# A delta rule kernel: order of work in the first and the last of eight heads

## The chip, the cores and the metric

The kernel runs on one core of one Trainium2 chip. The metric is the device time of one execution, in microseconds (us). Three runs of the kernel before gave 2688.31, 2688.33 and 2689.46 us; the median, 2688.33 us, is what the changed kernel is held against.

## The reference

The program is a trunk of two layers over 1024 tokens of width 1024: a gated DeltaNet mixer and a feed-forward block, then a gated linear attention mixer and a second feed-forward block. The change lies in the first mixer. Cut to that part, with the normalisation and the convolution named only:

```
qkv = silu(causal_depthwise_conv(p[..., :GDN_QKV], conv_w))       # 4 taps
q, k = l2_norm(q) * dk ** -0.5, l2_norm(k)
gc = cumsum(g)                                                     # in each chunk
decay = exp(where(causal, gc[i] - gc[j], -inf))
a = where(strict, (k * beta) @ k.T * decay, 0)
u, w = triangular_solve(a + eye, [v * beta, k * beta * exp(gc)])
qk = where(causal, q @ k.T * decay, 0)
for each chunk:                                                    # the scan
    v_new = u - w @ state
    o = (q * exp(gc)) @ state + qk @ v_new
    state = state * exp(gc_end) + (k * exp(gc_end - gc)).T @ v_new
o = rms_norm(o) * silu(z);  return o @ w_out
```

There are 8 heads of width 128. All arithmetic is float32; the large products are made from two rounded parts of each operand, as three matrix products.

## The kernel before, in words

One function, `gdn`, holds the mixer. It writes one program for each engine by hand, and the engines meet at semaphores; nothing reorders them, so the order of the code is the order of the queues. Each program runs `body(0)`, a loop of `body(h)` for heads 1 to 6, `body(7)` and `after(8)`. `peeled(h)` is true for head 0 and `final(h)` for head 7, so code under them is in one head only.

A head needs four projections of the input: keys, queries, values and the gate z. Each is a 1024x1024 weight tile in SBUF. SyncE loads it (`load(h, k)`), ScalarE rounds it to the high part (`high(h, k)`), GpSimd makes the low part (`split(h, k)`), and TensorE multiplies. TensorE's share is cut into pieces called fills: `fill(h, n)` is 6 matmuls of 512 columns. Fills 8k to 8k+7 make projection k of head h in PSUM (`pa`), four fills for each half of the tokens; projection 0 is the queries, 1 the values, 2 the next head's keys, 3 the gate z. (Head 0's fills -8 to -1 are its own keys; fills 0 to 7 its queries.) The first fill of each half waits until ScalarE has evicted that half of `pa` (`evict(h, k, half)`, semaphore `s_u`).

Beside the fills run the steps of the delta rule:

- VectorE convolves the keys in four taps (`conv`), ScalarE applies silu, TensorE turns them by token (`keys_by_token`), ScalarE squares them and copies them (`key_squares`), VectorE sums, ScalarE takes the root (`key_deviation`), and VectorE makes factors and multiplies the decay matrix (`key_chain`). TensorE multiplies the keys with themselves (`key_products`); VectorE makes the coupling matrix `aT` from both (`coupling_matrix`).
- The decay matrix starts from the row sums of the log decays. TensorE turns them (`decay_rows`), VectorE copies them (`cumT`), SyncE stores them to memory and loads them back, spread over all partitions (`load_columns`), and ScalarE takes two exponentials (`decay_exps`).
- The triangular inverse: GpSimd copies small blocks of `aT` (`near_blocks`), VectorE inverts them in some 25 small steps (`near_turned` to `near_back`), GpSimd spreads the result (`spread`, tiles `first` and `firstT`). Then three joins double the block: TensorE makes `coupled(h, n)`, ScalarE copies it (`m1_copies(h, n)`), TensorE makes `joined(h, n)`, VectorE subtracts (`join(h, n)`).
- Then query-key products, values by token, the product with w, and the next head's keys.

In head 7 the gate z takes the place of projection 2. Its tile `zc` still holds the output of head 6 until a DMA has stored it, so `evict(7, 2, 0)` waits for that store (semaphore `s_ost`).

Of the kernel before, what the change touches and what calls it, by code (L numbers as in the profile page):

```python
# [1144 lines left out]
GDN_TAPS = 4  # L1145
# [302 lines left out]
def gdn(nc, consts, w_in, w_gates, conv_w, a_log, dt_bias, o_gain, x_hi, x_lo, x_raw, mixed, cum_rows, w_out, x_in, x_out,  # L1448
# [3 lines left out]
    with ctx:  # L1452
# [128 lines left out]
        def peeled(h):  # L1581
            return isinstance(h, int) and h == 0
# [181 lines left out]
        def _(act):  # L1764
# [60 lines left out]
            def scan(h, projects, scans):  # L1825
                beside = {} if projects else tail_beside()
                if projects:
                    beside = {0: lambda: high(h, 1),
                              1: lambda: evict(h, 0, 0),
                              3: lambda: (evict(h, 0, 1), high(h, 2)),  # L1830
                              5: lambda: evict(h, 1, 0)}
# [44 lines left out]
            def prepare(h):  # L1876
# [14 lines left out]
                act.activation(stdq[:, :], ssq[:, :], ACT.Sqrt, bias=eps[:, 0:1]).then_inc(s_qstd, 1)  # L1891
                evict(h, 2, 0)
                m1_copies(h, 1)
                if not peeled(h):
                    silu(vT, 3 * h + 3)
# [44 lines left out]
            evict(0, -1, 1)  # L1940
            decay_exps_of_gates()
            silu(kT, 1)
            decay_exps(0)
            key_squares(0)
            key_deviation(0)
# [28 lines left out]
        def _(dve):  # L1974
# [17 lines left out]
            def conv_q(h, some):  # L1992
                conv(qT, u[1], 3 * h, halves(h, 0, 1), some)
# [138 lines left out]
            def scan(h, projects, scans):  # L2132
                beside = {}
                if projects:
# [7 lines left out]
                    if peeled(h):  # L2142
                        beside[0] = lambda: (coupling_matrix(h), conv_q(h, (1, 2, 3)))
                        beside[4] = lambda: near_joined(h, True)
                        del beside[6]
                for n in range(NT):
# [79 lines left out]
            def make_gates():  # L2226
# [31 lines left out]
                                  gates[:, :, G_CUM, :], ALU.subtract).then_inc(s_gr, 1)  # L2258
                dve.wait_ge(s_cumTp, 1)
                dve.tensor_copy(cumT[:, :], cumT_ps).then_inc(s_cumT, 1)  # L2260

            make_gates()
            dve.wait_ge(s_taps, 32)
            dve.wait_ge(s_set, 1)
            conv(kT, u[0], 1, halves(0, -1, 1), range(GDN_TAPS))
            dve.wait_ge(s_gates, 1)
# [23 lines left out]
        def _(pe):  # L2290
# [124 lines left out]
            def prepare(h):  # L2415
# [4 lines left out]
                if peeled(h):  # L2420
                    fill(h, *range(16, 24))
                pe.wait_ge(s_first, 2 * h + 2)
# [16 lines left out]
                coupled(h, 1)  # L2439
                some(20)  # L2440
                joined(h, 1)
                some(21, 22)
                coupled(h, 2)
                some(23)
                joined(h, 2)
# [810 lines left out]
```

## Time and profile before

| what | value |
|---|---|
| median of three runs | 2688.33 us |
| the profiled execution's own time | 2685.92 us |
| its span | 2683.9 us |
| mean granted TensorE clock | 0.991 of full speed |
| TensorE busy in matmuls | 2599.2 us (97%) |
| VectorE, GpSimd, ScalarE busy | 61%, 44%, 42% |
| first head, first projection to the loop over heads | about 31 to 131 us |
| last head, after its share of the scan, to the tail | about 638 to 681 us |

The profiled execution took 2.4 us less than the median; 2.0 us of its time lie outside the span. In a row of the timeline the first number is the start, the second the duration (of all instructions of a merged row, from the first's start to the last's end), both in us from the start of the span; then come the engine, the line, the operation, the tiles and the shape. What stands in square brackets is the time that the engine sat idle ahead of it, and what ended that.

### The profile page before, as it was taken

What the parts mean: (1) busy time and instruction counts of PE and PEld (TensorE: products, weight loads), DVE (VectorE), ACT (ScalarE), POOL (GpSimd) and SP (SyncE); (2) the same over time, 40 slices, a digit from 0 to 9 for tenths busy, and PEclk for the clock granted to TensorE, in tenths of its full rate; (3) what the DMA queues carried; (4) which work ended last, traced back from release to release, by engine and by line L of the source; (5) the groups of instructions that cost most, each with busy time, mean ns of one, the idle gap of its engine ahead of it and who ended that gap; (6) DMA issues with size and microseconds to landing.
All of it is one profiled execution on the core that took longest, in us unless ns stands there. A gap on an engine that the chain in (4) does not pass through costs nothing. (4 is left out here: it accounts for less than half of the span.)

```text
span 2683.9 us, 34327 instructions
## 1 busy us (share of the span) xinstructions
PE 2599.2 (97%) x12821; PEld 2156.9 (80%) x12821; DVE 1636.2 (61%) x1740; ACT 1115.2 (42%) x1645; POOL 1179.1 (44%) x721
## 2 busy tenths in 40 slices
PE   6999999999989999999999999999989999999998
PEld 5788888888778888888888688888878888888887
DVE  5677666676168666665455658557448666665454
ACT  6445545544443443433244334434533443433242
POOL 3444333434404778784443111111413877774442
PEclk9999999999999999999999999999999999999999
DMA  3111011111432222225554111012522222234553
GB/s 120 35 38 47 31 39 47 42 36 42 124 114 101 79 85 79 87 80 168 174 175 135 61 36 48 23 55 69 160 87 78 87 71 94 71 105 154 169 189 113
DMA packets 84541, 238.07 MB, mean 89 GB/s; under 512 B 8928, under 2 KB 22816, under 8 KB 84416
## 3 DMA queue, kind: packets, MB, share of 16 engines
q1 hardware_dynamic: 84416, 236.39, 26.6%
q8 instruction: 80, 1.31, 0.2%
q14 instruction: 45, 0.37, 0.0%
HBM read 189.66 MB, written 46.69 MB: 88 GB/s over the span
## 5 line engine op out<-in xcount | busy, mean ns | idle before, releaser
L391 POOL TENSOR_TENSOR f_wlo<-f_raw,f_whi 128x512 fp32r<-128x512 f32 (+1 forms) x210 | 426.5, 2032 | 499.4 <-ACT f_whi L432 499.4
L703 DVE TENSOR_TENSOR f_hlo<-f_hraw,f_hhi 128x512 fp32r<-128x512 f32 x88 | 182.1, 2075 | 200.9 <-ACT f_hhi L490 200.9
L432 ACT ACTIVATE f_whi<-f_raw 128x512 fp32r<-128x512 f32 (+1 forms) x210 | 171.9, 834 | 274.5 <-PE f_value L75 252.7
L391 POOL TENSOR_TENSOR f_wlo<-f_sums,f_whi 128x512 fp32r<-128x512 f32 x144 | 188.2, 1317 | 39.8 <-ACT f_whi L432 39.8
L432 ACT ACTIVATE f_whi<-f_sums 128x512 fp32r<-128x512 f32 x144 | 90.3, 627 | 270.7 <-POOL f_sums L397 270.7
L73 PE MATMUL f_value<-x_hi,f_whi 128*128 128x512 f32 x416 | 162.6, 391 | 1.6 <-POOL f_wlo L391 1.6
L74 PE MATMUL f_value<-x_lo,f_whi 128*128 128x512 f32 x416 | 162.6, 391 | 0.0
L75 PE MATMUL f_value<-x_hi,f_wlo 128*128 128x512 f32 x416 | 162.5, 391 | 0.0
L73 PE MATMUL f_part<-f_whi,f_hhi 128*128 128x512 f32 x352 | 137.9, 392 | 0.0
L75 PE MATMUL f_part<-f_whi,f_hlo 128*128 128x512 f32 x352 | 137.5, 391 | 0.0
L74 PE MATMUL f_part<-f_wlo,f_hhi 128*128 128x512 f32 x352 | 137.1, 389 | 0.0
L1685 POOL TENSOR_TENSOR g_wlo_first<-g_raw_first,g_whi_first 128x1024 fp32r<-128x1024 f32 x15 | 36.7, 2447 | 203.9 <-ACT g_whi_first L1770 203.9
L698 DVE TENSOR_TENSOR f_kept<-f_part,f_kept 128x512 f32<-128x512 f32 x72 | 49.8, 692 | 108.7 <-ACT f_kept L482 103.2
L2694 POOL TENSOR_TENSOR l_wlo<-l_raw,l_whi 128x1024 fp32r<-128x1024 f32 x12 | 29.3, 2445 | 195.3 <-ACT l_whi L2723 195.3
L73 PE MATMUL banks<-x_hi,g_whi 128*128 128x512 f32 x256 | 109.1, 426 | 6.2 <-POOL g_wlo L1685 6.2
L73 PE MATMUL banks<-x_hi,g_whi_first 128*128 128x512 f32 x256 | 110.1, 430 | 3.9 <-POOL g_wlo_first L1685 3.9
L75 PE MATMUL f_part<-x_hi,f_wlo 128*128 128x512 f32 x288 | 112.5, 390 | 0.0
L74 PE MATMUL f_part<-x_lo,f_whi 128*128 128x512 f32 x288 | 112.5, 390 | 0.0
L73 PE MATMUL f_part<-x_hi,f_whi 128*128 128x512 f32 x288 | 112.4, 390 | 0.0
L474 ACT ACTIVATE f_gate<-f_gate 128x1024 f32<-128x1024 f32 x44 | 46.7, 1062 | 148.5 <-DVE f_gate L689 148.5
L75 PE MATMUL banks<-x_hi,g_wlo_first 128*128 128x512 f32 x256 | 101.0, 395 | 0.0
L74 PE MATMUL banks<-x_lo,g_whi_first 128*128 128x512 f32 x256 | 100.9, 394 | 0.0
(539 smaller groups left out, 7652.2 us busy)
## 6 DMA issues: line engine op xcount, KB each, us to landing
f_raw<-in_ffn_w_up SPq DMA_DIRECT2D x88, 512.0 KB, 3.6
f_raw<-in_ffn_w_down SPq DMA_DIRECT2D x88, 512.0 KB, 3.6
hidden<-f_hid SPq DMA_DIRECT2D x44, 512.0 KB, 2.8
f_hraw<-hidden SPq DMA_DIRECT2D x88, 256.0 KB, 3.9
g_raw_first<-in_gdn_w_in SPq DMA_DIRECT2D x16, 512.0 KB, 3.6
g_raw<-in_gdn_w_in SPq DMA_DIRECT2D x16, 512.0 KB, 4.2
f_xt<-x_mid SPq DMA_DIRECT2D x16, 512.0 KB, 4.8
l_raw_first<-in_gla_w_in SPq DMA_DIRECT2D x12, 512.0 KB, 3.6
```

Source lines behind the costliest of these rows:

```text
L73: pe.matmul(out, w_hi, x_hi, start=first, stop=False)
L74: pe.matmul(out, w_hi, x_lo, start=False, stop=False)
L75: return pe.matmul(out, w_lo, x_hi, start=False, stop=last)
L391: pool.tensor_tensor(part_of(w_lo, k), source, part_of(w_hi, k).bitcast(F32), ALU.subtract) \
L432: act.activation(part_of(w_hi, k), source, ACT.Copy).then_inc(s_hi, 1)
L474: act.activation(gate[:, :], gate[:, :], ACT.Silu).then_inc(s_silu, 1)
L698: dve.tensor_tensor(out, psum, kept_part, ALU.add).then_inc(s_comb, 1)
L703: dve.tensor_tensor(h_lo[d % FFN_SLOTS][:, :], h_raw[d % HIDDEN_RAWS][:, :], plain32(h_hi[d % FFN_SLOTS][:, :]), ALU.subtract).then_inc(s_ ...
L1685: pool.tensor_tensor(w_lo[s][:, :], raw[s][:, :], w_hi[s][:, :].bitcast(F32), ALU.subtract) \
L2694: pool.tensor_tensor(w_lo[s][:, :], raw[s][:, :], w_hi[s][:, :].bitcast(F32), ALU.subtract) \
```

## The change

Six edits, all in `gdn`. In head 0: (1) VectorE's four taps for the keys are cut in two pairs, and the copy of the decay rows stands between them. (2) ScalarE's `high(0, 1)`, the rounding of the value weights, stands ahead of the silu of the keys; before, it stood after `key_deviation`. (3) `key_squares(0)` stands ahead of `decay_exps(0)`. (4) On VectorE two of the three remaining query taps move from behind the coupling matrix to behind `near_back`. (5) On TensorE fills 20 to 23 move from ahead of the joins to between them. In head 7: (6) ScalarE's copies for the second join stand ahead of the gate's first eviction.

```diff
--- before.py
+++ after.py
@@ -1825,7 +1825,7 @@
             def scan(h, projects, scans):
                 beside = {} if projects else tail_beside()
                 if projects:
-                    beside = {0: lambda: high(h, 1),
+                    beside = {0: lambda: None if peeled(h) else high(h, 1),
                               1: lambda: evict(h, 0, 0),
                               3: lambda: (evict(h, 0, 1), high(h, 2)),
                               5: lambda: evict(h, 1, 0)}
@@ -1889,8 +1889,11 @@
                     high(h, 3)
                 act.wait_ge(s_qss, h + 1)
                 act.activation(stdq[:, :], ssq[:, :], ACT.Sqrt, bias=eps[:, 0:1]).then_inc(s_qstd, 1)
-                evict(h, 2, 0)
+                if not final(h):
+                    evict(h, 2, 0)
                 m1_copies(h, 1)
+                if final(h):
+                    evict(h, 2, 0)
                 if not peeled(h):
                     silu(vT, 3 * h + 3)
                 if final(h):
@@ -1939,9 +1942,10 @@
             gate_exps()
             evict(0, -1, 1)
             decay_exps_of_gates()
+            high(0, 1)
             silu(kT, 1)
+            key_squares(0)
             decay_exps(0)
-            key_squares(0)
             key_deviation(0)
 
             def body(h):
@@ -2140,9 +2144,8 @@
                               5: lambda: near_back(h),
                               6: lambda: conv_q(h, (2, 3))}
                     if peeled(h):
-                        beside[0] = lambda: (coupling_matrix(h), conv_q(h, (1, 2, 3)))
+                        beside[0] = lambda: (coupling_matrix(h), conv_q(h, (1,)))
                         beside[4] = lambda: near_joined(h, True)
-                        del beside[6]
                 for n in range(NT):
                     if scans and n < NT - 1:
                         update_state(h - 1, n)
@@ -2256,13 +2259,14 @@
                 dve.drain()
                 dve.tensor_tensor(g_abs[:, :, :], total_ps.rearrange("p (h c) -> p h c", h=H),
                                   gates[:, :, G_CUM, :], ALU.subtract).then_inc(s_gr, 1)
-                dve.wait_ge(s_cumTp, 1)
-                dve.tensor_copy(cumT[:, :], cumT_ps).then_inc(s_cumT, 1)
 
             make_gates()
             dve.wait_ge(s_taps, 32)
             dve.wait_ge(s_set, 1)
-            conv(kT, u[0], 1, halves(0, -1, 1), range(GDN_TAPS))
+            conv(kT, u[0], 1, halves(0, -1, 1), (0, 1))
+            dve.wait_ge(s_cumTp, 1)
+            dve.tensor_copy(cumT[:, :], cumT_ps).then_inc(s_cumT, 1)
+            conv(kT, u[0], 1, halves(0, -1, 1), (2, 3))
             dve.wait_ge(s_gates, 1)
             key_chain(0)
 
@@ -2418,7 +2422,7 @@
                         fill(h, *fills)
 
                 if peeled(h):
-                    fill(h, *range(16, 24))
+                    fill(h, *range(16, 20))
                 pe.wait_ge(s_first, 2 * h + 2)
                 pe.wait_ge(s_at, h + 1)
                 coupled(h, 0)
@@ -2437,11 +2441,11 @@
                 else:
                     pe.wait_ge(s_qsq, h + 1)
                 coupled(h, 1)
-                some(20)
+                fill(h, 20)
                 joined(h, 1)
-                some(21, 22)
+                fill(h, 21, 22)
                 coupled(h, 2)
-                some(23)
+                fill(h, 23)
                 joined(h, 2)
                 fill(h, 24)
                 query_key_products(h)
```

ScalarE at the start of head 0, before the loop over heads, with what each instruction waits for (`g_kT` keys, `g_decay` and `g_fromstart` the two exponentials, `g_aT<-g_pm` the squares, `g_whi_first` the rounded value weights). Before:

```order
L1792 ACT_TABLE_LOAD
L1792 ACTIVATE g_kT<-g_kT 128x1024 [waits g_conv_done]
L1796 ACT_TABLE_LOAD
L1796 ACTIVATE g_decay<-g_decay 128x1024 [waits g_decay_exponent_made]
L1800 ACTIVATE g_fromstart<-g_columns 128x1024 [waits g_decay_by_columns_loaded]
L1806 ACTIVATE g_aT<-g_pm 128x1024 [waits g_keys_by_token_in_psum]
L1809 ACTIVATE g_kt<-g_pm 128x1024
L1813 ACT_TABLE_LOAD
L1813 ACTIVATE g_stdk<-g_ssk,eps 128x8 [waits g_key_squares_summed]
L1770 ACTIVATE g_whi_first<-g_raw_first 128x1024 [waits g_projection_half_done,g_w_raw_first]
L1784 ACTIVATE g_u<-banks 128x512 [waits g_projection_half_done]
```

The same place in the changed kernel:

```order
L1770 ACTIVATE g_whi_first<-g_raw_first 128x1024 [waits g_projection_half_done,g_w_raw_first]
L1792 ACT_TABLE_LOAD
L1792 ACTIVATE g_kT<-g_kT 128x1024 [waits g_conv_done]
L1806 ACTIVATE g_aT<-g_pm 128x1024 [waits g_keys_by_token_in_psum]
L1809 ACTIVATE g_kt<-g_pm 128x1024
L1796 ACT_TABLE_LOAD
L1796 ACTIVATE g_decay<-g_decay 128x1024 [waits g_decay_exponent_made]
L1800 ACTIVATE g_fromstart<-g_columns 128x1024 [waits g_decay_by_columns_loaded]
L1813 ACT_TABLE_LOAD
L1813 ACTIVATE g_stdk<-g_ssk,eps 128x8 [waits g_key_squares_summed]
L1784 ACTIVATE g_u<-banks 128x512 [waits g_projection_half_done]
```

The rounding of the weights, with its wait for the weight's DMA, went from the tenth row to the first, and the table load for silu now stands behind it; the two exponentials went behind the squares and the copy of the keys, and the eviction of the queries stays behind all of them.

VectorE between the coupling matrix of head 0 and the first small transpose, and at the end of the small inverse (`g_widerow` and `g_back` belong to the inverse, `g_qT` is the query convolution). Before:

```order
L2057 TENSOR_TENSOR g_aT<-g_pm,g_decay 128x1024 [waits g_key_products_done]
L1986 SCALAR_TENSOR_TENSOR g_qT<-g_u,g_taps,g_qT 128x1024 [waits g_projection_half_evicted]
L1986 SCALAR_TENSOR_TENSOR g_qT<-g_u,g_taps,g_qT 128x1024 x2
L2073 STREAM_TRANSPOSE g_widerow<-g_near 128x512 [waits g_near_blocks_copied]
...
L2129 STREAM_TRANSPOSE g_back<-g_widerow 128x16x16x2
L2129 STREAM_TRANSPOSE g_back<-g_rowsT 128x16x16x2
L2184 TENSOR_TENSOR g_inv<-g_first,g_pt 128x512 [waits g_join_products_done]
```

In the changed kernel:

```order
L2061 TENSOR_TENSOR g_aT<-g_pm,g_decay 128x1024 [waits g_key_products_done]
L1990 SCALAR_TENSOR_TENSOR g_qT<-g_u,g_taps,g_qT 128x1024 [waits g_projection_half_evicted]
L2077 STREAM_TRANSPOSE g_widerow<-g_near 128x512 [waits g_near_blocks_copied]
...
L2133 STREAM_TRANSPOSE g_back<-g_widerow 128x16x16x2
L2133 STREAM_TRANSPOSE g_back<-g_rowsT 128x16x16x2
L1990 SCALAR_TENSOR_TENSOR g_qT<-g_u,g_taps,g_qT 128x1024 [waits g_projection_half_evicted]
L1990 SCALAR_TENSOR_TENSOR g_qT<-g_u,g_taps,g_qT 128x1024
L2187 TENSOR_TENSOR g_inv<-g_first,g_pt 128x512 [waits g_join_products_done]
```

Two of three query taps went behind the last small transpose, ahead of the first join.

ScalarE in head 7 (`g_stdq` the query norms, `g_zc` the gate, `g_m` the copies for the second join, `g_vT` the silu of the values). Before:

```order
L1891 ACTIVATE g_stdq<-g_ssq,eps 128x8 [waits g_query_squares_summed]
L1781 ACT_TABLE_LOAD [waits g_output_stored]
L1781 ACTIVATE g_zc<-banks 128x512 [waits g_projection_half_done]
L1868 ACTIVATE g_m<-g_pm 128x512 [waits g_coupling_product_done] x2
L1792 ACTIVATE g_vT<-g_vT 128x1024 [waits g_conv_done]
```

In the changed kernel:

```order
L1891 ACTIVATE g_stdq<-g_ssq,eps 128x8 [waits g_query_squares_summed]
L1868 ACTIVATE g_m<-g_pm 128x512 [waits g_coupling_product_done] x2
L1781 ACT_TABLE_LOAD [waits g_output_stored]
L1781 ACTIVATE g_zc<-banks 128x512 [waits g_projection_half_done]
L1792 ACTIVATE g_vT<-g_vT 128x1024 [waits g_conv_done]
```

The two copies went ahead of the table load that waits for the store.

## Rows read from the trace of the kernel before

**Rows 1.** The page: busy time, share of the span and instructions of each engine.
```profile
PE 2599.2 (97%) x12821; PEld 2156.9 (80%) x12821; DVE 1636.2 (61%) x1740; ACT 1115.2 (42%) x1645; POOL 1179.1 (44%) x721
```
**Rows 2.** Waits of TensorE, 30 to 130 us: total, times, longest.
```profile
PE g_pt L2402 <- ACT g_m L1868: 1.5, 1, 1.5
...
PE g_pm L2385 <- DVE g_invT L2185: 0.5, 1, 0.5
```
**Rows 3.** Timeline of ScalarE in the first head: start, duration, engine, line, tiles.
```profile
54.79 1.06 ACT L1792 ACTIVATE g_kT<-g_kT 128x1024 f32<-128x1024 f32 x1 [4.78 <-DVE g_kT L1986]
...
57.54 1.06 ACT L1796 ACTIVATE g_decay<-g_decay 128x1024 f32<-128x1024 f32 x1 [0.40 <-DVE g_decay L2024]
...
59.46 1.00 ACT L1806 ACTIVATE g_aT<-g_pm 128x1024 f32<-128x1024 f32 x1
...
62.68 0.30 ACT L1813 ACTIVATE g_stdk<-g_ssk,eps 128x8 f32<-128x8 f32 x1
...
64.31 0.68 ACT L1787 ACTIVATE g_qT<-banks,g_taps 128x512 f32<-128x512 f32 x1
```
**Rows 4.** Timeline of SyncE's queue: issue of the value weights.
```profile
52.08 0.44 SPq L1613 DMA_DIRECT2D g_raw_first<-in_gdn_w_in  x1
```
**Rows 5.** DMA issues, 52.06 to 52.5 us: count, KB, us from issue to landing.
```profile
g_raw_first<-in_gdn_w_in SPq DMA_DIRECT2D x1, 512.0 KB, 4.7
```
**Rows 6.** Timeline of VectorE in the first head.
```profile
49.51 0.28 DVE L2260 COPY g_cumT<-g_pt 64x128 f32<-64x128 f32 x1 [2.22 <-PE g_pt L2477]
...
50.73 4.02 DVE L1986 SCALAR_TENSOR_TENSOR g_kT<-g_u,g_taps,g_kT 128x1024 f32<-128x1024 f32 x3
...
65.15 1.23 DVE L2057 TENSOR_TENSOR g_aT<-g_pm,g_decay 128x1024 f32<-128x1024 f32 x1
...
73.22 0.71 DVE L2073 STREAM_TRANSPOSE g_widerow<-g_near 128x512 f32<-128x512 f32 x1 [1.51 <-POOL g_near L1710]
...
87.66 1.11 DVE L2129 STREAM_TRANSPOSE g_back<-g_rowsT 128x512 f32<-128x512 f32 x1
```
**Rows 7.** Timeline of GpSimd in head 0 (two rows) and head 1 (two rows).
```profile
67.45 5.73 POOL L1710 TENSOR_TENSOR g_near<-g_aT,ones 32x256 f32<-32x256 f32 x4 [0.16 <-issue]
...
89.74 1.89 POOL L1717 TENSOR_TENSOR g_firstT<-g_back,g_inquarter 128x1024 f32<-128x1024 f32 x1
...
137.81 3.33 POOL L1710 TENSOR_TENSOR g_near<-g_aT,ones 32x256 f32<-32x256 f32 x4 [0.24 <-issue]
...
159.01 2.88 POOL L1717 TENSOR_TENSOR g_firstT<-g_back,g_inquarter 128x1024 f32<-128x1024 f32 x1
```
**Rows 8.** Timeline of TensorE in the first head.
```profile
55.90 1.09 PE L2338 MATMUL g_pm<-ident,g_kT 128*128 128x128 f32 x8 [0.94 <-ACT g_kT L1792]
...
67.35 0.66 PE L73 MATMUL banks<-x_hi,g_whi_first 128*128 128x512 f32 x1 [3.87 <-POOL g_wlo_first L1685]
...
91.69 2.05 PE L2387 MATMUL g_pm<-g_first,g_nearcT 128*128 128x128 f32 x16 [0.69 <-POOL g_firstT L1717]
...
109.14 1.22 PE L2399 MATMUL g_pt<-g_invT,g_m 128*64 128x64 f32 x16
```
**Rows 9.** Busy us of each engine in a stretch, granted clock, DMA share, GB/s.
```profile
67.00:71.00 4.00, 3.65 (x9) 2.89 (x10) 3.85 (x3) 0.00 (x0) 3.56 (x4) 0.57 0.43 131
```
**Rows 10.** Timeline of ScalarE in the last head.
```profile
655.50 1.28 ACT L1781 ACT_TABLE_LOAD   x1 [5.59 <-DMA mixed<-g_zc]
...
657.28 1.08 ACT L1868 ACTIVATE g_m<-g_pm 128x512 f32<-128x512 f32 x2
```
**Rows 11.** Timeline of TensorE in the last head.
```profile
657.93 0.72 PE L2402 MATMUL g_pt<-g_m,g_invT 128*128 128x128 f32 x2 [2.62 <-ACT g_m L1868]
...
663.15 0.48 PE L73 MATMUL banks<-x_hi,g_whi 128*128 128x512 f32 x1
...
665.98 1.89 PE L2385 MATMUL g_pm<-g_inv,g_cT 128*128 128x64 f32 x16
```
**Rows 12.** Timeline of VectorE in the last head.
```profile
659.54 0.16 DVE L2203 COPY g_cd<-g_hg 128x8 f32<-128x8 f32 x1
```

## The prediction

> **What bounds the kernel now.** I read the page first. TensorE is busy for 97% of the span and no other engine for more than 61% [rows 1]. So an edit that only reorders other engines can pay only where TensorE stands still, and it costs where it makes TensorE stand still. The edits touch two places, so the next views were the list of TensorE's waits and the timelines of both. In the first head TensorE waits 3.87 us for the low part of the value weights (the wait in the row of 67.35), 0.69 us for the spread inverse (the row of 91.69) [rows 8], and between the joins 1.5 us for ScalarE's copies and 0.5 us for VectorE [rows 2]. In the last head it waits 2.62 us for the copies of the second join [rows 11], because ScalarE stood 5.59 us at the store of the gate's tile and then loaded a table ahead of them [rows 10]. The third thing to see is the granted clock: after the 3.87 us of idling it is 0.57 on average from 67 to 71 us, which is the 1.2 GHz level for about 3.4 us and the 2.4 GHz level after it [rows 9]. So such an idle stretch costs 4 x (1 - 0.57) = 1.7 us more than itself. Waits of 0.9 and 1.5 us were not followed by this.
>
> **Edit 1, taps around the copy (head 0).** VectorE waits 2.22 us for the decay rows and makes its four taps after that; the last three take 4.02 us, 1.34 us each [rows 6]. Two taps now stand in the wait (2.2 us for a scaling and one tap), the copy stays at 49.6 us, and the other two end at 52.6 us instead of 54.75. The decay rows' way through memory starts when it did. The gain would be 2.1 us for the silu of the keys, if ScalarE were free.
>
> **Edit 2, the weights first.** It is not free. The value weights are issued at 52.08 us [rows 4] and land 4.7 us later [rows 5], at 56.8 us. SyncE's queue is not changed; this issue stands behind the decay rows' store and load. Behind the waiting `high(0, 1)` now stands the silu of the keys, and behind that all of the key chain on TensorE, VectorE and GpSimd. Rounding takes 1.0 us (all ScalarE operations over 1024 columns take 1.0 to 1.1 us [rows 3]), so it ends at 57.8; then comes silu's table load of 1.28 us (the duration in [rows 10]), which before was done ahead of need; silu ends at 60.2 us instead of 55.85. That is 4.3 us late, although its input is 2.1 us early.
>
> **Edit 3, squares ahead of exponentials.** TensorE has been idle since 54.95 us (55.90 less the 0.94 us wait [rows 8]), 5.2 us in all, so I take the low clock for the turn of the keys: 1.9 us instead of 1.09 [rows 8]. Squares and copy run from 62.1 to 64.1 us. Before, the exponentials ran while TensorE turned the keys; now they stand on the path between the copy and the root: a table load, two exponentials of 1.0 us [rows 3], a table load, the root. 64.1 + 1.3 + 2.0 + 1.3 + 0.3 = 69.0 us, instead of 62.68 + 0.30 = 63.0. The coupling matrix follows 2.2 us behind the root, as before: it starts at 71.15 us instead of 65.15 [rows 6]. The key chain is 6.0 us late.
>
> **Edit 4, two query taps moved back.** GpSimd's near blocks took 5.73 us with three taps beside them, and 3.33 us in head 1 with hardly any beside them [rows 7]. With one tap I take the middle, 4.5 us. Also, GpSimd could start only at 67.45 us, 1.1 us after the coupling matrix was done, since it was splitting weights; that split is over by 60.2 us now. So the blocks run from 72.4 to 76.9 us, and the first small transpose comes at 76.95 instead of 73.22 [rows 6]: 3.7 us late of the 6.0. The rest of the small inverse has the same neighbours as before. But two taps now run beside `spread`. In head 1, where this is so, `firstT` took 2.88 us instead of 1.89 [rows 7]: 1.0 us lost. The first coupling starts at 91.69 + 3.7 - 0.1 + 1.0 = 96.3 us: **4.6 us late.** The bounds of this step: 3.6 us (no loss beside the taps) and 6.5 us (GpSimd stands still for whole taps of 1.34 us: one at the blocks, 4.7 us instead of 4.5, and two at `firstT`, 2.7 us instead of 1.0).
>
> **Edit 5, fills among the joins.** First, TensorE before them. Fill 8 writes over the queries' first half, so it waits for the eviction, which stands behind the root on ScalarE: 69.0 + 1.0 = 70.0 us instead of 64.31 + 0.68 = 65.0 [rows 3]. The low part of the weights, which set 67.35 us before, is ready at 60.2 and no longer matters. Behind the turn come fills 6 and 7, partly at the low clock, to 65.4 us, and 2.0 us of key products (as long as the like-shaped coupling [rows 8]), to 67.4 us, so the wait of 3.87 becomes one of 2.6 us, 2.7 us later, and I leave the low clock there. A fill costs 1.4 us (two from 663.15 to 665.98 [rows 11]). Fills 8 to 19 are 12 x 1.4 + 1.7 = 18.5 us: TensorE is done at 88.5 us and then idles for 7.8 us. Before, it had all 16 fills done and waited 0.69 us. The four fills that went cannot fill this hole. The first coupling then runs at the low clock, which the kernel before doesn't do there: **1.7 us.** The four fills, 5.6 us, now stand between the couplings and joins, where TensorE waited 1.5 + 0.5 us [rows 2] and lost some 0.2 us at hand-overs: **3.4 us** are added. Everything behind the joins (VectorE's value taps, the next keys) hangs on the third join at 109.14 [rows 8] and moves with it.
>
> Head 0: 4.6 + 1.7 + 3.4 = **9.7 us slower.** Nothing later takes it back, because TensorE carries fills without slack through heads 1 to 6.
>
> **Edit 6, copies ahead of the gate (head 7).** The copies wait for the second coupling only, which stands ahead of fill 20, so TensorE goes on at 657.93 - 2.62 = 655.3 us, right behind fill 20. The wait of 2.62 us goes. With it goes the low clock: the join's 5.2 us (657.93 to 663.15 [rows 11]) become 3.5. What is late next is VectorE: its value taps and small steps end at 659.70 us [rows 12], and its two subtraction halves of 1.3 us then end at 661.1 and 662.4. TensorE, at 658.8 + 2 x 1.4 = 661.6 us, wants the first half at once and the second 0.85 us later. Both are there, just. So the next coupling starts at 661.7 instead of 665.98: **4.3 us faster.** The loads of the output weights wait for TensorE's steps and move with it. The bounds: 2.6 us (the wait alone) and 4.5.
>
> **The sum.** 9.7 - 4.3 = 5.4 us slower. Against the profiled execution's own 2685.92 us that is 2691.3 us; the median of the runs is 2.4 us above that execution, so I forecast **2693.7 us**. What can be told from no change is about 0.2%, 5.4 us: my sum lies right at that bound.
>
> **Rivals.**
> A. *The keys are not held up* (the other side). If the value weights land before the first head's taps end, at some 52 us, the silu runs at 52.7 us. The point that decides is the landing: each us after 51.6 us is a us on the chain. Then the root is where it was (63 us), GpSimd is free for the near blocks, and the first coupling starts 1.3 us early. The low clock and the four fills stay (1.7 + 3.4): 3.8 - 4.3 = -0.5, 2687.8 us. With rival C's 1.7 and 1.0 on top it is 2685.1; even that is within 0.2%. For it speaks only that the load is a plain one; against it the issue at 52.08 us [rows 4].
> B. *The last head gives less.* VectorE is late at the coupling by as much as the join is faster, and only the wait goes: 9.7 - 2.6 = 7.1, 2695.4 us. For it speaks how narrow the hand-over is (661.7 against 661.1 and 662.4).
> C. *The clock stays up in head 0.* No low clock at the turn of the keys (0.8) nor at the first coupling (1.7), and `spread` loses nothing (1.0): 9.7 - 3.5 - 4.3 = 1.9, 2690.2 us. Against it: the row of 67.35 [rows 8, 9].
> D. *GpSimd is shut out by the taps, not slowed.* Then `firstT` waits for both taps, 2.7 us, instead of losing 1.0: 5.4 + 1.7 = 7.1, 2695.4 us. Head 1's row speaks against it: 2.88 us [rows 7]. The Trainium skill has such a rule, on its page "SBUF — State Buffer", section "Who interferes with whom": a VectorE instruction with two inputs in SBUF and a GpSimd instruction that reads SBUF exclude each other, and the later one waits for the whole of the other. By that rule the move of the taps costs this 1.7 us more; by the row it doesn't, since GpSimd lost less than one tap.
>
> **How the numbers follow.** The forecast 0.44, B 0.18, C 0.20, A 0.10, D 0.06, and 0.02 for what I have not priced. The forecast is split about evenly by the bound. Slower by over 0.2%: 0.23 + 0.17 + 0.06 = 0.46, and 0.01 from C: 0.47. Faster by over 0.2%: 0.02 of A and the 0.02, 0.04. Within 0.2%: 0.49. The range runs from rival A's time to B and D with the upper bound of the first coupling (6.5 - 4.6 = 1.9 us) and some noise: 2687.5 to 2698 us. The forecast's own range is 2691 to 2696.
>
> **What would show it.** On ScalarE, `high(0, 1)` with a wait for the DMA until 56.8 us, and the silu of the keys at 59.1. On TensorE, the turn of the keys at 60.2 us, fill 8 at 70 with a wait on ScalarE instead of GpSimd, a wait of some 8 us before the first coupling at 96.3, and the third join at 118.8. In the last head, as stretches between rows: no wait between fill 20 and the join, the join in 3.5 us, and clock 1.0 there. The prediction is wrong if the silu starts before 56 us, or if TensorE reaches the first coupling without a long wait.

## The result, and the profile after

| | before | after |
|---|---|---|
| time, median (lowest to highest) | 2688.49 us (2684.97 to 2690.66), 20 runs | 2692.74 us (2690.18 to 2696.34), 20 runs |
| ratio | 1 | 1.0016 [1.0009, 1.0023] |
| span of the profiled execution | 2683.9 us | 2688.8 us |

The changed kernel is slower by 4.2 us [2.4, 6.2]; forecast were 5.4 us and 2693.7 us. The loss is real, since the interval lies above 1, and it is smaller than the 0.2% that I had named as the bound of what can be told.

The page of the profile after hardly differs from before [rows 1]. Its line of busy times per engine:
```profile
PE 2601.2 (97%) x12821; PEld 2158.6 (80%) x12821; DVE 1637.6 (61%) x1740; ACT 1115.7 (41%) x1645; POOL 1180.8 (44%) x721
```
TensorE is busy for 2.0 us more (2601.2 against 2599.2) in a span that is 4.9 us longer, so it stands still for 2.9 us more; part of the busy time is matmuls at a lower clock, below. What changed is where it stands still. TensorE's waits after, from 30 to 130 us, the stretch of [rows 2] (us in total, times, longest):
```profile
PE g_pm L2391 <- POOL g_firstT L1717: 7.6, 1, 7.6
...
PE g_pt L2406 <- ACT g_m L1868: 0.3, 1, 0.3
```
The joins' wait for ScalarE fell from 1.5 to 0.3 us [rows 2]: the fills between the joins did hide it. The first line is the hole that they left, 7.6 us before the first coupling.

One correction belongs to all that follows. The mixer's first load is issued by SyncE at 32.62 us after and at 31.97 us before, 0.65 us later for no reason in the change. A time of after in the first head is therefore read less 0.65 us when it stands beside one of before or of the prediction.

ScalarE in the first head, in order of time (start, us, engine, line, operation, out<-in, idle time ahead and what ended it):
```profile
57.40 1.06 ACT L1770 ACTIVATE g_whi_first<-g_raw_first 128x1024 fp32r<-128x1024 f32 x1 [8.11 <-DMA g_raw_first<-in_gdn_w_in]
58.47 1.28 ACT L1792 ACT_TABLE_LOAD   x1
59.76 1.06 ACT L1792 ACTIVATE g_kT<-g_kT 128x1024 f32<-128x1024 f32 x1
...
69.45 0.30 ACT L1813 ACTIVATE g_stdk<-g_ssk,eps 128x8 f32<-128x8 f32 x1
70.13 0.68 ACT L1787 ACTIVATE g_qT<-banks,g_taps 128x512 f32<-128x512 f32 x1
```
This answers [rows 3]. (As the rows show, what is loaded and rounded is 128x1024 elements, 512 KB [rows 5]: one head's share of a projection, not a tile of 1024x1024.) The engine stands 8.11 us at the landing of the value weights, with the silu of the keys behind it in its queue. The keys' taps had long been done. VectorE of the same stretch, with the same columns:
```profile
50.17 0.28 DVE L2268 COPY g_cumT<-g_pt 64x128 f32<-64x128 f32 x1
50.55 2.65 DVE L1990 SCALAR_TENSOR_TENSOR g_kT<-g_u,g_taps,g_kT 128x1024 f32<-128x1024 f32 x2
...
71.92 1.23 DVE L2061 TENSOR_TENSOR g_aT<-g_pm,g_decay 128x1024 f32<-128x1024 f32 x1
...
77.41 0.71 DVE L2077 STREAM_TRANSPOSE g_widerow<-g_near 128x512 f32<-128x512 f32 x1 [2.38 <-POOL g_near L1710]
```
Here is edit 1 doing what it says: the copy [rows 6] no longer has idle time ahead of it, and the last two taps end at 53.20 us (52.55 corrected) instead of 54.75. Then nothing uses the keys for 6.56 us, from 53.20 to 59.76. The coupling matrix comes 6.1 us later than in [rows 6], 71.27 against 65.15.

GpSimd of the same stretch, against [rows 7]:
```profile
73.23 4.14 POOL L1710 TENSOR_TENSOR g_near<-g_aT,ones 32x256 f32<-32x256 f32 x4 [12.35 <-DVE g_aT L2061]
...
93.80 2.87 POOL L1717 TENSOR_TENSOR g_firstT<-g_back,g_inquarter 128x1024 f32<-128x1024 f32 x1
```
The near blocks became 1.59 us shorter with two taps fewer beside them, and `firstT` 0.98 us longer with those taps beside it. TensorE, against [rows 8]:
```profile
60.87 1.97 PE L2342 MATMUL g_pm<-ident,g_kT 128*128 128x128 f32 x8 [5.28 <-ACT g_kT L1792]
...
70.95 0.47 PE L73 MATMUL banks<-x_hi,g_whi_first 128*128 128x512 f32 x1 [2.25 <-ACT g_qT L1787]
...
96.73 3.46 PE L2391 MATMUL g_pm<-g_first,g_nearcT 128*128 128x128 f32 x16 [7.57 <-POOL g_firstT L1717]
...
104.13 1.04 PE L2342 MATMUL g_pm<-ident,g_qT 128*128 128x128 f32 x8
...
119.49 1.15 PE L2403 MATMUL g_pt<-g_invT,g_m 128*64 128x64 f32 x16
```
The first coupling took 2.05 us before [rows 8] and 3.46 now. The windows show why (length, busy us of PE, PEld, DVE, ACT and POOL, granted clock, DMA share, GB/s):
```profile
60.00:62.00 2.00, 1.13 (x6) 1.13 (x7) 0.00 (x0) 0.82 (x1) 0.88 (x1) 0.50 0.04 8
73.00:76.00 3.00, 3.00 (x9) 2.35 (x8) 1.93 (x2) 1.06 (x1) 2.49 (x3) 0.53 0.37 150
97.00:100.00 3.00, 3.00 (x16) 3.00 (x16) 0.76 (x1) 2.21 (x4) 2.99 (x1) 0.55 0.00 0
100.00:103.00 3.00, 2.74 (x24) 2.55 (x23) 0.46 (x1) 0.89 (x2) 0.00 (x0) 1.00 0.02 5
```
A clock of 0.50 is the 1.2 GHz level, 1.00 the 2.4 GHz level. The head has three stretches at the lower level where it had one [rows 9]: at the turn of the keys and the fills behind it, at the first value fills (73 to 76 us, the place of the one before), and at the first coupling. The second costs nothing here, since TensorE waits for 7.57 us behind those fills.

The last head. TensorE after, against [rows 11]:
```profile
662.38 2.05 PE L2391 MATMUL g_pm<-g_inv,g_cT 128*128 128x128 f32 x16
...
665.66 0.38 PE L2406 MATMUL g_pt<-g_m,g_invT 128*128 128x128 f32 x2
...
669.15 0.48 PE L73 MATMUL banks<-x_hi,g_whi 128*128 128x512 f32 x1
...
671.99 2.14 PE L2389 MATMUL g_pm<-g_inv,g_cT 128*128 128x64 f32 x16
...
675.50 1.15 PE L2403 MATMUL g_pt<-g_invT,g_m 128*64 128x64 f32 x16
```
and ScalarE, against [rows 10]:
```profile
663.58 0.60 ACT L1868 ACTIVATE g_m<-g_pm 128x512 f32<-128x512 f32 x1 [3.17 <-PE g_pm L2391]
...
667.09 1.28 ACT L1781 ACT_TABLE_LOAD   x1 [2.02 <-DMA mixed<-g_zc]
```
The copies now go ahead of the gate's table load, the join's row at 665.66 us has no idle time, and the join ends 3.49 us later (669.15) instead of 5.22 us [rows 11]. From the second coupling to the third join it is 13.12 us (662.38 to 675.50) instead of 17.39.

Where the time went, as stretches that start with each mixer's own first load: head 0 up to its query-key product +9.63 us (79.81 to 89.44), heads 1 to 6 +0.24, the last head's couplings and joins -4.27, and the tail behind them -0.56. That makes +5.05 us. The spans differ by 4.9 us: 0.65 us of the late start come on top, and some 0.8 us come back between 1440 and 1571 us, at the second mixer's boundary, where both kernels run the same code.

### The profile page after: what moved, and what is told of

Its sections match the earlier page's. It is cut to its first block and busy times, and to the rows that moved or that the text cites. A ratio compares the mean times of both kernels' runs of the same rounds, so it can differ in the third digit from the quotient of the medians.

```text
span 2688.8 us, 34327 instructions
## 1 busy us (share of the span) xinstructions
PE 2601.2 (97%) x12821; PEld 2158.6 (80%) x12821; DVE 1637.6 (61%) x1740; ACT 1115.7 (41%) x1645; POOL 1180.8 (44%) x721
```

## The experiments

Three numbers of each trace are compared, since whole spans carry a drift of about 1 us through heads 1 to 6. *First coupling* and *query-key* are the starts of these two steps of head 0, in us from the mixer's first load; *last head* is the stretch from its second coupling to its third join. The ratios are to the kernel before, timed beside each.

| | ratio | first coupling | query-key | last head |
|---|---|---|---|---|
| before | 1 | 59.72 | 79.81 | 17.39 |
| after | 1.0016 [1.0009, 1.0023] | 64.11 | 89.44 | 13.12 |
| 1. after, edit 2 undone | 0.9994 [0.9985, 1.0003] | 58.79 | 84.13 | 13.12 |
| 2. before + edit 2 | 1.0018 [1.0009, 1.0027] | 62.64 | 84.30 | 15.79 |
| 3. before + edit 6 | 0.9980 [0.9971, 0.9989] | 59.67 | 79.79 | 13.12 |
| 4. before + edit 5 | 1.0022 [1.0013, 1.0031] | 59.63 | 84.97 | 15.77 |
| 5. after, weights loaded early | 0.9996 [0.9987, 1.0005] | 58.92 | 84.29 | 13.12 |
| 6. before + edit 4 | 1.0035 [1.0021, 1.0049] | 69.92 | 89.92 | 18.18 |
| 7. before + edits 1, 2, 6, early load | 0.9980 [0.9970, 0.9989] | 58.45 | 78.54 | 13.11 |
| 8. as 7, query taps behind the spread | 0.9968 [0.9957, 0.9980] | 56.83 | 78.39 | 13.14 |

**1. The changed kernel with the weights' rounding back behind the silu.**
```
-                    beside = {0: lambda: None if peeled(h) else high(h, 1),
+                    beside = {0: lambda: high(h, 1),
...
-            high(0, 1)
             silu(kT, 1)
```


> The changed kernel with edit 2 undone: the rounding of the value weights stands behind the root of the key norms again, all other edits stay. My theory (the silu of the keys stood behind the landing of the value weights): silu starts at about 52.7 us, the root of the key norms is ready at about 63, the coupling matrix starts at about 65.2, the first coupling at about 91.1 (1.6 us gained at the near blocks, 1.0 lost at the spread). TensorE still waits some 5 us there and starts at the low clock (1.7), and the four fills still add 3.4: first coupling to third join some 22 us. Against the kernel before: 4.5 - 4.3 = +0.2 us, ratio 1.000. Rival (the order of squares and exponentials alone delays the chain, whatever the weights do): the coupling matrix starts at 69 us or later and the ratio stays at 1.0015.

2686.03 us over 11 runs, ratio 0.9994 [0.9985, 1.0003]: level with before. ScalarE:
```profile
51.76 1.06 ACT L1792 ACTIVATE g_kT<-g_kT 128x1024 f32<-128x1024 f32 x1 [2.57 <-DVE g_kT L1989]
...
61.62 0.30 ACT L1813 ACTIVATE g_stdk<-g_ssk,eps 128x8 f32<-128x8 f32 x1
```
TensorE:
```profile
89.95 3.75 PE L2390 MATMUL g_pm<-g_first,g_nearcT 128*128 128x128 f32 x16 [5.47 <-POOL g_firstT L1717]
```
The silu waits for VectorE's taps again. From the mixer's first load (issued at 31.16 us here) it starts at 20.60 us, where after has 27.14 and before 22.82 [rows 3], so edit 1 does bring the 2.2 us that it should. The root gets little of it: 30.46 us, against 30.71 before. At the first coupling and at the query-key product alike, 5.3 us of that is left (64.11 - 58.79, 89.44 - 84.13). That is what edit 2 costs in the changed kernel, more than the whole loss. The rest of head 0's loss, 4.32 us, stays: the wait of 5.47 us and the coupling at 3.75 us are still there. It is 5.25 us behind the start of the coupling, where experiment 4 has the same, less 0.93 us by which the coupling comes early.

**2. The weights first, alone, in the kernel before.**
```
-                    beside = {0: lambda: high(h, 1),
+                    beside = {0: lambda: None if peeled(h) else high(h, 1),
...
+            high(0, 1)
             silu(kT, 1)
             decay_exps(0)
             key_squares(0)
```


> The kernel before with edit 2 alone: the rounding of the value weights stands ahead of the silu of the keys, exponentials ahead of squares as before, all taps and fills as before. My theory: silu starts at 59.1 us behind the landing of the weights, then the exponentials run while TensorE turns the keys, and the root is ready at about 67 us (4.0 us late, not 6.0). GpSimd is free, so the near blocks start 1.1 us nearer to the coupling matrix: the first coupling at about 94.6 us, 2.9 us late, with or without 1.7 us of low clock: ratio 1.0011 to 1.0017. Rival (the wait for the weights is hidden, since TensorE gets its value weights earlier): fill 8 starts before 67.35 us and the ratio is 1.000 or below.

2692.70 us over 11 runs, ratio 1.0018 [1.0009, 1.0027]. ScalarE and then TensorE:
```profile
59.26 1.06 ACT L1792 ACTIVATE g_kT<-g_kT 128x1024 f32<-128x1024 f32 x1
...
66.77 0.30 ACT L1813 ACTIVATE g_stdk<-g_ssk,eps 128x8 f32<-128x8 f32 x1
```
```profile
94.80 3.25 PE L2388 MATMUL g_pm<-g_first,g_nearcT 128*128 128x128 f32 x16 [3.36 <-POOL g_firstT L1717]
...
663.61 0.49 PE L2403 MATMUL g_pt<-g_m,g_invT 128*128 128x128 f32 x2 [2.63 <-ACT g_m L1868]
```
With all taps still beside the near blocks, the first coupling comes 2.9 us late, and it runs at the low clock (its window from 95 to 98 us has a granted clock of 0.57): 1.6 us more at the query-key product, 4.49 us in all. From the mixer's first load (at 32.16 us here) the silu starts at 27.10 us and the root at 34.61; after, they are at 27.14 and 36.83. This kernel has the exponentials under TensorE's turn of the keys and the other has them behind the copy, so edit 3 costs 2.2 us at the root. (No run takes edit 3 alone back, so its share at the first coupling is not measured.) Experiment 1 shows the same loss: with edit 1's 2.2 us in hand, its root comes only 0.25 us earlier than before.

**3. The last head alone, in the kernel before.**
```
-                evict(h, 2, 0)
+                if not final(h):
+                    evict(h, 2, 0)
                 m1_copies(h, 1)
+                if final(h):
+                    evict(h, 2, 0)
```


> The kernel before with edit 6 alone: in the last head the copies for the second join stand ahead of the gate's eviction. My theory: 4.3 us less, 2.6 of it the wait and 1.7 the low clock behind it; ratio 0.9984. The stretch from second coupling to third join takes 13.1 us instead of 17.4. Rival (only the wait goes): 2.6 us, ratio 0.9990. Rival (it is lost again in the tail, whose loads are bound by the DMA): ratio 1.000.

2682.35 us over 11 runs, ratio 0.9980 [0.9971, 0.9989], so 5.5 us faster. TensorE:
```profile
652.10 2.05 PE L2390 MATMUL g_pm<-g_inv,g_cT 128*128 128x128 f32 x16
...
665.22 1.15 PE L2402 MATMUL g_pt<-g_invT,g_m 128*64 128x64 f32 x16
```
ScalarE:
```profile
655.75 1.28 ACT L1781 ACT_TABLE_LOAD   x1 [0.96 <-DMA mixed<-g_zc]
```
The stretch is 13.12 us, to the hundredth what it is after. The gate's table load still waits for the store, but nobody waits for the gate. In this stretch the edit is worth 4.27 us with or without the others; the whole times give 5.5, and the interval (3.0 to 7.8 us) holds both.

**4. The four fills among the joins, alone, in the kernel before.**
```
-                    fill(h, *range(16, 24))
+                    fill(h, *range(16, 20))
...
-                some(20)
+                fill(h, 20)
                 joined(h, 1)
-                some(21, 22)
+                fill(h, 21, 22)
                 coupled(h, 2)
-                some(23)
+                fill(h, 23)
```


> The kernel before with edit 5 alone: in head 0 fills 20 to 23 stand among the joins instead of ahead of them. My theory: the first coupling starts at 91.7 us as before, since the spread inverse sets it, but TensorE waits some 6 us there and then starts at the low clock (1.7 us lost), and the four fills add 3.4 us up to the third join: 5.1 us slower, ratio 1.0019. Rival (fills among joins fill the joins' waits, as in the other heads, and cost nothing): the first coupling to the third join takes 17.5 us as before, ratio 1.000. Rival (only the fills cost, the clock stays up): 3.4 us, ratio 1.0013.

2693.62 us over 11 runs, ratio 1.0022 [1.0013, 1.0031]. TensorE:
```profile
92.31 3.79 PE L2387 MATMUL g_pm<-g_first,g_nearcT 128*128 128x128 f32 x16 [5.96 <-POOL g_firstT L1717]
```
The first coupling starts where it started before (59.63 against 59.72), behind 5.96 us of idling. The query-key product is 5.16 us late: low clock plus four fills less the waits that they hide, 5.1 by the prediction's terms (1.7 + 3.4). So the fills lose time because they leave a place where they were free, and because the idling that they leave there is followed by the low clock.

**5. The changed kernel with the value weights loaded early** (SyncE issues them at 34.34 us).
```
+            sp.wait_ge(s_lo, begun(0, 1 - SLOTS))
+            load(0, 1)
...
-                    sp.wait_ge(s_lo, begun(h, k - SLOTS))
-                    load(h, k)
+                    if not (peeled(h) and k == 1):
+                        sp.wait_ge(s_lo, begun(h, k - SLOTS))
+                        load(h, k)
```


> The changed kernel with all six edits, but SyncE issues the value weights at about 36 us, ahead of its wait for the decay rows, instead of at 52 us. My theory: the rounding runs at about 49 us without a wait for the DMA, silu of the keys starts right behind the taps (2.1 us earlier than in the kernel before), the root of the key norms is ready at about 62, the near blocks start 0.1 us behind the coupling matrix, and the first coupling comes 1.0 us earlier than with the weights back behind the root. Then the changed kernel loses its 5 us: ratio to before 0.999 to 0.9997. Rival (the order of ScalarE's queue costs, not the landing): silu starts after 56 us and the ratio is 1.0015.

2687.37 us over 11 runs against 2688.77, ratio 0.9996 [0.9987, 1.0005]. ScalarE, VectorE and GpSimd where the silu starts:
```profile
48.03 1.06 ACT L1773 ACTIVATE g_whi_first<-g_raw_first 128x1024 fp32r<-128x1024 f32 x1 [0.16 <-issue]
...
54.03 1.06 ACT L1795 ACTIVATE g_kT<-g_kT 128x1024 f32<-128x1024 f32 x1 [3.64 <-DVE g_kT L1993]
```
```profile
49.13 4.87 DVE L1993 SCALAR_TENSOR_TENSOR g_kT<-g_u,g_taps,g_kT 128x1024 f32<-128x1024 f32 x2
```
```profile
49.17 2.39 POOL L1688 TENSOR_TENSOR g_wlo_first<-g_raw_first,g_whi_first 128x1024 fp32r<-128x1024 f32 x1 [9.48 <-ACT g_whi_first L1773]
```
With the wait at the landing gone, as in rival A, the changed kernel is level with before. The late issue on SyncE, at 52.08 us before [rows 4] and 52.73 us after, was indeed what held the keys. From the mixer's first load (at 31.21 us here) the silu starts at 22.82 us, as before. I had expected the silu 2.1 us earlier and a further 1.0 us over experiment 1, from GpSimd being free for the near blocks. Both were missed; the first coupling is 0.13 us later than there (58.92 against 58.79). GpSimd's split now runs beside the last two key taps, and these take 4.87 us instead of 2.65. The gain was eaten one step earlier.

**6. Two query taps moved back, alone, in the kernel before.**
```
-                        beside[0] = lambda: (coupling_matrix(h), conv_q(h, (1, 2, 3)))
+                        beside[0] = lambda: (coupling_matrix(h), conv_q(h, (1,)))
                         beside[4] = lambda: near_joined(h, True)
-                        del beside[6]
```


> The kernel before with edit 4 alone: two query taps behind the small inverse, all fills ahead of the joins as before. My theory: edit 4 without edit 5 is far worse than either in the changed kernel. Fill 20 waits for the eviction of the values' second half, which stands on ScalarE behind the silu of the queries, and that waits for the two taps. The taps end at about 92 us, the eviction at 94.5, fills 20 to 23 take 5.5 + 1.7 us (low clock), and the first coupling starts at about 101.7 instead of 91.7: 10 us slower, ratio 1.0037. Rival (only the neighbours of GpSimd change): 1.5 us gained at the near blocks, 1.0 lost at the spread, ratio 0.9998 to 1.000.

2698.04 us over 5 runs, ratio 1.0035 [1.0021, 1.0049]. TensorE:
```profile
94.57 0.77 PE L73 MATMUL banks<-x_hi,g_whi 128*128 128x512 f32 x1 [8.70 <-ACT g_vT L1787]
...
102.20 1.95 PE L2386 MATMUL g_pm<-g_first,g_nearcT 128*128 128x128 f32 x16
...
669.29 0.79 PE L2401 MATMUL g_pt<-g_m,g_invT 128*128 128x128 f32 x2 [3.53 <-ACT g_m L1868]
```
ScalarE:
```profile
92.30 1.06 ACT L1792 ACTIVATE g_qT<-g_qT 128x1024 f32<-128x1024 f32 x1 [14.80 <-DVE g_qT L1986]
...
93.74 0.68 ACT L1787 ACTIVATE g_vT<-banks,g_taps 128x512 f32<-128x512 f32 x1
```
Alone it is the worst edit. Fill 20 needs a bank whose eviction stands on ScalarE behind the silu of the queries, and that silu waits for the last query tap (14.80 us of ScalarE's idle time). With the fills still ahead of the first coupling, TensorE waits 8.70 us at fill 20 and the coupling comes 10.2 us late. (Its last head takes 18.18 us instead of 17.39, because the wait for the copies there, in the row of 669.29, is 3.53 us instead of 2.62.) So edit 5 is the other half of edit 4: it takes those fills from in front of the coupling. The two have to be priced together.

**7. The kernel before with edits 1, 2 and 6 and the early load** (the early load as in experiment 5, edits 3, 4 and 5 left out).

> The kernel before with edits 1, 2 and 6 and the value weights issued at about 36 us: a version meant to beat both. Exponentials ahead of squares, all query taps and all fills where they were. My theory: the chain to the root is as long as before, but GpSimd has split the weights long ago, so the near blocks start 1.1 us nearer to the coupling matrix, and fill 8 starts when the queries are evicted, 2.3 us earlier. TensorE then waits some 3.6 us at the first coupling and has the low clock there (1.3 us): -1.1 + 1.3 - 4.3 = -4.1 us, ratio 0.9985. Rival (TensorE's earlier fills count in full): -6 us, ratio 0.9977.

2682.24 us over 11 runs, ratio 0.9980 [0.9970, 0.9989]. TensorE:
```profile
90.97 2.05 PE L2395 MATMUL g_pm<-g_first,g_nearcT 128*128 128x128 f32 x16 [3.35 <-POOL g_firstT L1720]
```
With the landing out of the way, head 0 gains 1.27 us at both steps instead of losing. The idle time before the coupling is the same as in experiment 2, 3.35 against 3.36 us, but the coupling takes 2.05 us, not 3.25: here the clock stayed at the upper level (granted 1.00 from 91 to 94 us), where I had expected the lower one.

**8. As 7, with the query taps behind the spread.** VectorE waits for GpSimd's `spread` before the last two query taps; ScalarE's eviction and the first join's copies go ahead of the silu of the queries; seven of the eight late fills stay ahead of the first coupling, and one goes where the join waits.
```
+                        beside[6] = lambda: (dve.wait_ge(s_first, 2 * h + 2), conv_q(h, (2, 3)))
...
-                silu(qT, 3 * h + 2)
+                if not peeled(h):
+                    silu(qT, 3 * h + 2)
...
+                if peeled(h):
+                    silu(qT, 3 * h + 2)
...
+                    fill(h, *range(16, 23))
...
+                if peeled(h):
+                    fill(h, 23)
```


> As the version before (edits 1, 2 and 6, early load), with two query taps behind the spread of the inverse (VectorE waits for the spread first, so that they don't slow it), ScalarE's eviction of the values and its copies for the first join ahead of the silu of the queries, fills 16 to 22 ahead of the joins and fill 23 in the wait ahead of the second join. My theory: near blocks 1.6 us shorter and 1.1 us earlier, no loss at the spread: first coupling 2.7 us early, low clock there (1.3), fill 23 hidden in the 1.5 us wait: -2.7 + 1.3 - 4.3 = -5.7 us, ratio 0.9979. Rival (the silu of the queries comes late for the turn of the queries and eats the gain): ratio 0.9985 or more, with a wait of TensorE before the turn of the queries.

2679.86 us over 7 runs, ratio 0.9968 [0.9957, 0.9980]: the fastest of all, ahead of both kernels. GpSimd, VectorE and TensorE:
```profile
87.30 1.89 POOL L1720 TENSOR_TENSOR g_firstT<-g_back,g_inquarter 128x1024 f32<-128x1024 f32 x1
```
```profile
89.29 4.66 DVE L1996 SCALAR_TENSOR_TENSOR g_qT<-g_u,g_taps,g_qT 128x1024 f32<-128x1024 f32 x2 [3.04 <-POOL g_firstT L1720]
```
```profile
89.24 3.57 PE L2398 MATMUL g_pm<-g_first,g_nearcT 128*128 128x128 f32 x16 [4.18 <-POOL g_firstT L1720]
```
Without taps beside it `firstT` takes 1.89 us again, as in head 0 before [rows 7], and the coupling is 2.9 us earlier than before. Its 4.18 us of idling is followed by the low clock, which gives back half of that: the query-key product is 1.42 us early. With the last head's 4.25 us that makes the 5.7 us that I had expected. The whole times say more: 8.9 us here against 5.5 us for the last head's edit alone. Each of these has an interval of more than 2 us on either side, and spans drift by about 1 us, so of the difference of 3.4 us I claim only the 1.42 that the stretch shows.

## Why the prediction was right

Its time, 2693.7 us, is 1.0 us above the median, and both terms of the sum are near the measured ones: +9.7 against +9.63 in the first head, -4.3 against -4.27 in the last. That the first is so near is in part luck: the first coupling came 4.39 us late where 4.6 were forecast, and what lies behind it cost 5.24 us where 5.1 were. Its steps one by one, with times of after less 0.65 us:

| step | forecast | measured |
|---|---|---|
| rounding of the value weights starts | 56.8 | 56.75 |
| silu of the keys starts | 59.1 | 59.11 |
| turn of the keys: start, us | 60.2, 1.9 | 60.22, 1.97 |
| root ready | 69.0 | 69.10 |
| coupling matrix | 71.15 | 71.27 |
| near blocks, us | 4.5 | 4.14 |
| first small transpose | 76.95 | 76.76 |
| `firstT`, us | 2.88 | 2.87 |
| fill 8: start, wait | 70.0, 2.6 | 70.30, 2.25 |
| first coupling: start, wait | 96.3, 7.8 | 96.08, 7.57 |
| third join | 118.8 | 118.84 |

- *The waiting instruction sets the silu.* Right. Experiment 1 takes the order back and experiment 5 the late landing; each alone brings the changed kernel level with before. It costs 5.3 us inside the changed kernel. The head is 4.32 us late without it, and the two make 9.63.
- *Rival A*, keys not held up, is what experiment 5 built: 2687.37 us where A said 2687.8. The two times are nearer than the mechanism: A had the silu 2.1 us early and a sum of -0.5 us, and by its stretches experiment 5 has the silu where it was and +0.2 us (4.48 - 4.27). In the changed kernel the landing rules A out.
- *Fills and the clock behind the coupling.* Forecast 3.4 + 1.7. From the first coupling to the turn of the queries after takes 7.40 us (96.73 to 104.13) and before 5.52 (91.69 to 97.21): 1.88 us more for the same work of TensorE, which ran at the lower clock up to about 100 us. From that turn to the third join it is 3.43 us more, which is the fills. Alone (experiment 4) it is 5.16 us at the query-key product.
- *Rival B* fell, by this row and the next on VectorE in the last head after:
```profile
670.31 0.69 DVE L2187 TENSOR_TENSOR g_inv<-g_inv,g_pt 128x512 f32<-128x512 f32 x1
...
671.68 0.69 DVE L2187 TENSOR_TENSOR g_inv<-g_inv,g_pt 128x512 f32<-128x512 f32 x1
```
The first half is there in time, the second begins at 671.68 us, and the coupling's row at 671.99 has no idle time ahead of it. The hand-over is as narrow as I said; the coupling itself takes 2.14 us instead of 1.89 [rows 11].
- *Rival C* fell: the turn of the keys and the first coupling both ran at the low level.
- *Rival D*: its price fell, its mechanism did not. `firstT` lost 0.98 us beside two taps, as in head 1, not 2.7. But the single taps show that GpSimd and VectorE did shut each other out (the last section): `firstT` lost only what was left of one tap. The prediction took head 1's loss of less than one tap as speaking against that; it had the right number for `firstT` from that row, and the wrong reading of it.

What was off. The near blocks came out 0.36 us shorter than the middle that I took. The rows before would have given it: three taps beside them cost 5.73 - 3.33 = 2.40 us, so one costs a third of that, 0.80, and not half; 3.33 + 0.80 = 4.13, and 4.14 was measured. Behind fill 8's wait of 2.25 us the low clock came later than at that place before: fill 8 itself took 0.47 us, and the window from 73 to 76 us shows 0.53. The tail behind the last head gave 0.56 us that I had not priced; its own stretch at the low clock is shorter after (0.65 on average from 684 to 688 us) than before (0.54 from 678 to 685 us). I can't say why. And the sum of traces is 5.05 us where the medians differ by 4.2 [2.4, 6.2], which the interval holds.

Left open: what decides whether the clock falls after 2 to 4 us of idling (below), and the 0.8 us that came back at the second mixer's boundary.

## What to carry to other kernels

An engine's queue runs in order, so before an instruction that waits for a load is put ahead of others, read when that load is issued and lands: here the rounding was moved ahead of a silu whose input was ready 6.6 us before it ran, and that cost 5.3 us. Issuing the load early removed this cost without touching the order.

Work that fills idle time is free only where the idle time is. Four fills moved from a hole of 6 to 8 us to places with 2 us of waits cost 5.2 us, 1.9 of it by the lower clock behind the hole.

Where an edit's two halves meet at a hand-over (here the late taps and the fills behind their eviction), price and try them together: one half alone cost 10.1 us, and the other alone 5.2.

## What the runs showed of the hardware

*Idle time and the clock.* The same idle time was followed by a lower clock in some kernels and not in others. Before the last head's second join, about 2.6 us of idling was followed by the low level in the kernel before [rows 11] and not in experiments 2 and 4, whose stretch to the third join is 15.79 and 15.77 us instead of 17.39. Before the first coupling, 3.36 us was followed by it (3.25 us for the coupling, experiment 2) and 3.35 us was not (2.05 us, experiment 7). A price for it is therefore a chance where the idling is 2 to 4 us; where the low level came at the first coupling, the way to the turn of the queries was 1.5 to 1.9 us longer (5.52 us before; 6.98 in experiment 8, 7.40 after). All of the first couplings behind 4.18 us or more took 3.46 to 3.79 us.

*VectorE and GpSimd together.* Two key taps took 4.87 us beside GpSimd's split and 2.65 alone, while the split took 2.39 us. `firstT` took 2.87 us with two query taps and 1.89 without. In experiment 8 two query taps took 4.66 us beside the GpSimd work that follows `spread`. Taken as sums, these look like a partial slowing of now one engine and now the other. The order of the instructions in the changed kernel says otherwise:
```profile
91.95 1.89 POOL L1717 TENSOR_TENSOR g_first<-g_back,g_inquarter 128x1024 f32<-128x1024 f32 x1 [10.71 <-DVE g_back L2133]
...
96.64 3.35 POOL L1699 TENSOR_TENSOR g_cT<-g_aT,masks 128x1024 f32<-128x1024 f32 x1
```
```profile
92.83 4.93 DVE L1990 SCALAR_TENSOR_TENSOR g_qT<-g_u,g_taps,g_qT 128x1024 f32<-128x1024 f32 x2
```
Taken singly, the two taps of the last row run from 92.83 to 94.93 us and from 95.00 to 97.76 us, and one alone takes 1.28. In the order of their starts:

| instruction | start, end | the other engine's, begun earlier, ends | from that end to its own | alone |
|---|---|---|---|---|
| `first`, GpSimd | 91.95, 93.84 | | | 1.89 |
| tap, VectorE | 92.83, 94.93 | 93.84 | 1.09 | 1.28 |
| `firstT`, GpSimd | 93.80, 96.67 | 94.93 | 1.74 | 1.89 |
| tap, VectorE | 95.00, 97.76 | 96.67 | 1.09 | 1.28 |
| `cT`, GpSimd | 96.64, 99.99 | 97.76 | 2.23 | 2.35 |

Each ends as if it had begun 0.1 to 0.2 us before the earlier one of the other engine ended, and `first`, which began alone, loses nothing. So in these pairs, two operands from SBUF on either side, the later instruction stood still for nearly all of the rest of the earlier one. In experiment 5 the first of the two late key taps takes 3.51 us and the second 1.28, so one tap carries the whole loss of 2.2 us beside a split of 2.39; in experiment 8 it is 3.30 and 1.28, beside 2.36. And the near blocks are longer by about 0.80 us for each tap beside them (3.33, 4.14 and 5.73 us with none, one and three).
